# Expert gate and up weights in 4 KB rows, half the contraction of both in one slab, and 512-column projections

## The chip, the core and the metric

The kernel runs on one core of one Trainium2 chip. The metric is the device time of one execution in microseconds (us). The kernel before takes 1487.6 us (median of three runs, 1486.89 to 1495.12).

The engines: TensorE (PE, with its weight loads as PEld), VectorE (DVE), ScalarE (ACT), GpSimd (POOL), and SyncE (SP), which issues nearly all transfers from HBM.

## What is computed

Two transformer blocks on 256 tokens of width 1024, in float32. The change lies in the last stage of the second block, a mixture of 32 experts in 4 groups of 8. Each token goes to one group, and there to two experts. Cut to this stage:

```python
def hier_moe(h, w_rg, b_rg, w_re, b_re, w_gate, w_up, w_down):
    ...
    combine = jax.nn.one_hot(g_idx, N_EXPERT_GROUPS, dtype=jnp.float32)[:, :, None] * (g_w * within)[:, None, :]
    out = jnp.zeros_like(hf)
    for g in range(N_EXPERT_GROUPS):
        a = jnp.einsum('nd,edf->nef', hf, w_gate[g])
        u = jnp.einsum('nd,edf->nef', hf, w_up[g])
        act = jax.nn.silu(a) * u * combine[:, g, :, None]
        out = out + jnp.einsum('nef,efd->nd', act, w_down[g])
```

Per expert the gate and the up weights are 1024 x 256 each and the down weights 256 x 1024: three times 1 MB in float32. `h` is the RMS-normed input; its gain is `ffn_norm_2`.

## The kernel before

**Precision by splitting.** Every float32 operand of a large product is split into a high part and a rest (both in the fp32r format), and a product is three matmuls: high x high, high x low, low x high (`mm3`, L456). Activations are kept split already (`Uh`/`Ul`, here `SUh`/`SUl`). Weights are split as they arrive.

**The slab pipeline.** All weights of the program go through one ring of three slots (`NSLOT`), each slab 128 partitions x 2048 words (1 MB), in two halves of 1024 words:
- SP loads a half into `raw` (L406) when DVE has finished the half that was there before (the `lo_done` wait, L404).
- ACT copies it to `whi` (L418) when it has landed and when PE has used up the slab that was in the slot (the `slab_used` wait, L413).
- DVE subtracts, `wlo = raw - whi` (L424).
- PE waits for both halves of `lo_done`, multiplies, and counts up `slab_used`.

Each engine runs its own program in the written order, so a wait holds back everything behind it on that engine.

**The expert stage.** The tokens of a group are first gathered into at most 128 columns per group: PE multiplies the normed input (`XNh`, `XNl`, L2232) by 0/1 selection matrices, ACT and DVE scale by the gain and split the result into `SUh`/`SUl` (L1364, L1822). Then 32 experts follow, with the slabs in the order gate 0, up 0, gate 1, up 1, down 0, gate 2, up 2, down 1, and so on. For each step `body(E)` of the three engines does this, in this order:
- PE (`pe_experts`, L689): transposes the hidden vectors of expert E-1 (`turn`), projects the gate slab of E into bank 4 and its up slab into bank 5 (`project`, 8 chunks of the contraction x 3 matmuls of 256 columns each), then runs the down product of E-1 (`down`, 12 matmuls of 512 columns).
- ACT (`act_experts`, L754): SiLU of the gate projection of E (L778), split of gate E+1 and up E+1 (4 halves, L418), a copy of the transposed hidden vectors (`hh`, L791), split of down E (2 halves).
- DVE (`dve_experts`, L801): the product with up and combine weight (L814), the rests of gate E+1 and up E+1 (4 halves, L424), `hl` (L825), the rests of down E.

The SiLU of E waits for the gate slab alone, which PE finishes one slab before the up slab:

```python
                    act.wait_ge(*reach("slab_used", b + 3 * E))
...
                act.activation(sgh[:, 0, 0:T], bank[4][:, 0:T], ACT.Silu).then_inc(S("moe_silu"), 1)
                more = kind != 3
                if more:
                    split_hi(b + 2, E)
                    split_hi(b + 3, E)
```

Of every group of 8 experts, the first two steps are written out and the other steps run in a hardware loop (`runs`, L676; for the last group its last step is written out too). At the start of groups 2, 3 and 4 the finished group's result is copied out, multiplied by the transposed selection matrices (`put_back`, L714) and added to `X` by POOL (L840); the last group's follows at the end.

## Time and profile before

| | before |
|---|---|
| median of 3 runs | 1487.6 us (1486.89 to 1495.12) |
| span of the profiled execution | 1485.9 us |
| PE busy | 1369.9 us (92%) |
| DVE busy | 934.3 us (63%) |
| ACT busy | 766.2 us (52%) |
| read from HBM | 261.17 MB |

The span runs from the first to the last instruction; the profiled execution's own device time is not listed beside it, and the span is 1.7 us below the median of the three runs. PE is busy throughout, but the program has many stages with other limits. The expert stage fills the last 314 us of the span.

### The profile page before, as it was taken

What the parts mean: (1) busy time and instruction counts of PE and PEld (TensorE: products, weight loads), DVE (VectorE), ACT (ScalarE), POOL (GpSimd) and SP (SyncE); (2) the same over time, 40 slices, a digit from 0 to 9 for tenths busy, and PEclk for the clock granted to TensorE, in tenths of its full rate; (3) what the DMA queues carried; (4) which work ended last, traced back from release to release, by engine and by line L of the source; (5) the groups of instructions that cost most, each with busy time, mean ns of one, the idle gap of its engine ahead of it and who ended that gap; (6) DMA issues with size and microseconds to landing.
All of it is one profiled execution on the core that took longest, in us unless ns stands there. A gap on an engine that the chain in (4) does not pass through costs nothing.

```text
span 1485.9 us, 25448 instructions
## 1 busy us (share of the span) xinstructions
PE 1369.9 (92%) x9776; PEld 1273.7 (86%) x9776; DVE 934.3 (63%) x1359; ACT 766.2 (52%) x1112; POOL 175.3 (12%) x135
## 2 busy tenths in 40 slices
PE   6999999979989999998898987989998899999997
PEld 6999989977789999998897777889998788888885
DVE  4555554564565555564497663674664688888885
ACT  4343345645544343455454555325643577777774
POOL 1211120101002111200200001420000000202021
PEclk9999999999999999999998999989997899999999
DMA  7656554542155555554433232315453299999995
GB/s 241 214 182 192 178 146 156 158 141 78 58 170 168 178 191 181 186 156 120 135 114 114 85 110 64 112 40 162 157 171 128 85 338 347 321 343 322 336 322 189
DMA packets 222158, 263.36 MB, mean 177 GB/s; under 512 B 14017, under 2 KB 204798, under 8 KB 221950
## 3 DMA queue, kind: packets, MB, share of 16 engines
q1 hardware_dynamic: 219520, 260.39, 54.4%
q10 hardware_dynamic: 2558, 1.86, 0.4%
q8 instruction: 55, 0.90, 0.2%
q14 instruction: 25, 0.20, 0.0%
HBM read 261.17 MB, written 1.05 MB: 176 GB/s over the span
## 4 chain that ended last, share of the span: by engine, by line
PE 55%; issue 24%; DVE 11%; ACT 6%; POOL 2%; DMA 1%; ACTq 0%; POOLq 0%; DVEq 0%
PE bank L458 17%; PE bank L459 16%; PE bank L460 16%; DVE sb_wlo L424 3%; POOL sb_X L840 1%; ACT sb_whi L418 1%; DVE sb_XC L1580 1%; PE bank L2180 1%; PE bank L553 1%; ACT sb_aw L1256 1%; DMA sb_pos<-in_positions 1%; DVE sb_aw L1612 1%; DVE sb_st L862 1%; ACT sb_XC L1227 0%; ACT sb_xn L513 0%
## 5 line engine op out<-in xcount | busy, mean ns | idle before, releaser
L424 DVE TENSOR_TENSOR sb_wlo<-sb_raw,sb_whi 128x1024 fp32r<-128x1024 f32 (+1 forms) x498 | 620.3, 1289 | 252.4 <-ACT sb_whi L418 251.8
L418 ACT ACTIVATE sb_whi<-sb_raw 128x1024 fp32r<-128x1024 f32 (+1 forms) x498 | 503.6, 1047 | 305.3 <-PE bank L460 243.9
L458 PE MATMUL bank<-sb_Uh,sb_whi 128*128 128x256 f32 x1216 | 350.7, 288 | 6.0 <-DVE sb_wlo L424 4.5
L459 PE MATMUL bank<-sb_Ul,sb_whi 128*128 128x256 f32 x1216 | 347.6, 286 | 0.0
L460 PE MATMUL bank<-sb_Uh,sb_wlo 128*128 128x256 f32 x1216 | 347.4, 286 | 0.0
L458 PEld LDWEIGHTS bank<-sb_Uh,sb_whi 128*128 128x128 f32 x1216 | 237.3, 195 | 11.4 <-issue 8.3
L459 PEld LDWEIGHTS bank<-sb_Ul,sb_whi 128*128 128x128 f32 x1216 | 237.5, 195 | 0.7
L460 PEld LDWEIGHTS bank<-sb_Uh,sb_wlo 128*128 128x128 f32 x1216 | 236.9, 195 | 0.0
L458 PE MATMUL bank<-sb_whi,sb_Uh 128*128 128x256 f32 (+3 forms) x560 | 162.0, 289 | 1.2 <-DVE sb_Ul L543 0.8
L459 PE MATMUL bank<-sb_wlo,sb_Uh 128*128 128x256 f32 (+3 forms) x560 | 161.4, 288 | 0.0
L460 PE MATMUL bank<-sb_whi,sb_Ul 128*128 128x256 f32 (+3 forms) x560 | 161.3, 288 | 0.0
L458 PE MATMUL bank<-sb_whi,sb_SUh 128*128 128x256 f32 x512 | 148.4, 290 | 6.0 <-DVE sb_wlo L424 4.0
L459 PE MATMUL bank<-sb_wlo,sb_SUh 128*128 128x256 f32 x512 | 144.5, 282 | 0.0
L460 PE MATMUL bank<-sb_whi,sb_SUl 128*128 128x256 f32 x512 | 144.4, 282 | 0.0
L458 PE MATMUL bank<-sb_whi,sb_hh 128*128 128x512 f32 x288 | 113.1, 393 | 1.2 <-DVE sb_hl L825 0.9
L458 PEld LDWEIGHTS bank<-sb_whi,sb_Uh 128*128 128x128 f32 x560 | 111.6, 199 | 2.5 <-issue 1.9
L459 PE MATMUL bank<-sb_wlo,sb_hh 128*128 128x512 f32 x288 | 112.7, 391 | 0.0
L460 PE MATMUL bank<-sb_whi,sb_hl 128*128 128x512 f32 x288 | 112.3, 390 | 0.0
L459 PEld LDWEIGHTS bank<-sb_wlo,sb_Uh 128*128 128x128 f32 x560 | 111.7, 199 | 0.0
L460 PEld LDWEIGHTS bank<-sb_whi,sb_Ul 128*128 128x128 f32 x560 | 111.5, 199 | 0.0
L458 PEld LDWEIGHTS bank<-sb_whi,sb_SUh 128*128 128x128 f32 x512 | 97.1, 190 | 13.3 <-DVE sb_wlo L424 12.2
L460 PEld LDWEIGHTS bank<-sb_whi,sb_SUl 128*128 128x128 f32 x512 | 97.2, 190 | 0.0
(392 smaller groups left out, 1928.6 us busy)
## 6 DMA issues: line engine op xcount, KB each, us to landing
sb_raw<-in_w_in SPq DMA_DIRECT2D x104, 512.0 KB, 4.4
sb_raw<-in_ffn_w_in SPq DMA_DIRECT2D x88, 512.0 KB, 4.6
sb_raw<-in_w_gate SPq DMA_DIRECT2D x64, 512.0 KB, 4.7
sb_raw<-in_w_up SPq DMA_DIRECT2D x64, 512.0 KB, 6.4
sb_raw<-in_w_down SPq DMA_DIRECT2D x64, 512.0 KB, 6.1
sb_raw<-in_ffn_w_out SPq DMA_DIRECT2D x44, 512.0 KB, 3.7
sb_raw<-in_w_out SPq DMA_DIRECT2D x16, 512.0 KB, 4.5
sb_raw<-in_w_ssd_branch SPq DMA_DIRECT2D x16, 512.0 KB, 4.7
```

The costliest lines, as they stand in the source:

```text
L418: nc.scalar.activation(whi[:, i % NSLOT, c], raw[:, i % NSLOT, c], ACT.Copy).then_inc(S("hi_done"), 1)
L424: nc.vector.tensor_tensor(wlo[:, i % NSLOT, c], raw[:, i % NSLOT, c], whi[:, i % NSLOT, c].bitcast(F32), ALU.subtract).then_inc(S("lo_done ...
L458: pe.matmul(o, lh, rh, start=start, stop=False, skip_group_check=True)
L459: pe.matmul(o, lh, rl, start=False, stop=False, skip_group_check=True)
L460: return pe.matmul(o, ll, rh, start=False, stop=stop, skip_group_check=True)
L553: last = pe.transpose(bank[4 + j][:, c * T + t * P:c * T + (t + 1) * P], xn[:, t, (2 * j + c) * P:(2 * j + c + 1) * P], ident)
L840: pool.tensor_tensor(xs_, xs_, PUT[:, part], ALU.add).then_inc(S("x_add"), 1)
L862: dve.tensor_reduce(stat(nm, 2 * H)[:, t * H:(t + 1) * H], scr[:, 0:H * d].rearrange("p (h d) -> p h d", d=d), AX, ALU.add).then_inc(S(nm ...
L1256: act.activation(aw[:, i % 3, lo:hi], aw[:, i % 3, lo:hi], ACT.Exp, bias=nmx[:, 2 * i + t:2 * i + t + 1], scale=HD ** -0.5, accum_out=sm[: ...
L1580: dve.scalar_tensor_tensor(XC[:, ch, s_:T], sgh[:, j % 2, c * T:(c + 1) * T - s_], gcol("conv_w_2", (TAPS - 1 - s_) * NX + ch), XC[:, ch, ...
L1612: dve.tensor_tensor_reduce(out=aw[:, i % 3, lo:hi], in0=bank[i % 3][:, lo:hi], in1=SELB[:, lo:hi], scale=1.0, scalar=-3e38, op0=ALU.add, o ...
L2180: last = pe.matmul(bank[4 + v % 2][:, h * SP:(h + 1) * SP], EM(2 * v + h // 4)[:, h % 4 * P:(h % 4 + 1) * P], Xd[:, v % 2, h * SP:(h + 1) ...
```

## The change

- **Which rows of a weight go to which partition.** Before, chunk k of the contraction holds rows 128k to 128k+127, one per partition, so that a partition gets a 1 KB piece of each chunk. Now partition p gets rows 8p to 8p+7 (`(p k) n`), which lie together in HBM: 8 KB, read as two runs of 4 KB.
- **What a slab holds.** Before, one slab is a gate and the next is an up. Now the first slab holds chunks 0 to 3 of gate (first half) and up (second half), and the next slab chunks 4 to 7 of both. Sizes, slots, halves and their number stay.
- **The projections.** A matmul now streams 256 gate columns and 256 up columns together, 512 in all, into bank 4: 12 matmuls per slab instead of 24. Bank 5 is not used. Both results are complete only at the end of the second slab, so the SiLU waits for it (`slab_used` one higher).
- **The gathered input.** Its chunk c must now hold features c, 8+c, 16+c, ...: the stationary operand of the gathering matmuls is read with a step of 8 words (`every`). The gain is needed in the same order, so ACT loads it once more, early in the program, as 8 words per partition (one more transfer on its queue), and waits for it before it scales `SUh`.

The down weights and everything ahead of this stage stay as they were.

```diff
+        at_rows = P + n_rows2
+        row_gain = lambda c: G[:, at_rows + c:at_rows + c + 1]
...
-        experts = lambda nm, k: a[nm].rearrange("o g e (k p) n -> (o g e) p k n", p=P)
-        wg, wu, wd = (experts(nm, 0) for nm in ("w_gate_2", "w_up_2", "w_down_2"))
-        slab_loop("moe", NE, lambda e: wg[e], lambda e: wu[e], lambda e: wd[e])
+        wg, wu = (a[nm].rearrange("o g e (p k) n -> (o g e) p (k n)", p=P) for nm in ("w_gate_2", "w_up_2"))
+        wd = a["w_down_2"].rearrange("o g e (k p) n -> (o g e) p k n", p=P)
+
+        def rows_of(e, j):
+            c = slice(j * SLAB // 2, (j + 1) * SLAB // 2)
+            return [wg[e][:, c], wu[e][:, c]]
+
+        slab_loop("moe", NE, lambda e: rows_of(e, 0), lambda e: rows_of(e, 1), lambda e: wd[e])
...
+            if isinstance(src, list):
+                for h, half in enumerate(src):
+                    if i >= NSLOT or q is not None:
+                        n = h + 1 if part_cols(i) == part_cols(i - NSLOT) else 2
+                        sp.wait_ge(*reach("lo_done", 2 * (i - NSLOT) + n + (0 if q is None else q * 6)))
+                    sp.dma_start(raw[:, i % NSLOT, h * SLAB // 2:(h + 1) * SLAB // 2], half).then_inc(S(f"raw_full{i % NSLOT}{h}"), 16)
+                return
...
+        every = lambda x, c: x.rearrange("p (q k) -> p k q", k=KD)[:, c]
...
             def project(j, i, E, u):
                 pe.wait_ge(*reach("lo_done", 2 * (i + 1) + 6 * E))
-                by_token(i, 4 + j, SUh[:, :, u], SUl[:, :, u], KD, 256, tiles=[0]).then_inc(S("slab_used"), 1)
+                wh, wl = (w[:, i % NSLOT, :].rearrange("p (m k n) -> p k m n", m=2, n=EH) for w in (whi, wlo))
+                for k in range(KD // 2):
+                    c = j * KD // 2 + k
+                    last = mm3(bank[4][:, :], SUh[:, c, u], SUl[:, c, u], wh[:, k], wl[:, k], c == 0, c == KD - 1)
+                last.then_inc(S("slab_used"), 1)
...
-                if first:
-                    act.wait_ge(*reach("slab_used", b + 1))
-                else:
-                    act.wait_ge(*reach("slab_used", b + 3 * E))
+                act.wait_ge(*reach("slab_used", (b + 2) if first else b + 1 + 3 * E))
...
-                dve.scalar_tensor_tensor(sgh[:, 1, 0:T], sgh[:, 0, 0:T], w, bank[5][:, 0:T], ALU.mult,
+                dve.scalar_tensor_tensor(sgh[:, 1, 0:T], sgh[:, 0, 0:T], w, bank[4][:, T:2 * T], ALU.mult,
                                          ALU.mult).then_inc(S("moe_mul"), 1)
...
+            act.dma_start(G[:, at_rows:at_rows + KD], a["ffn_norm_2"][0].rearrange("(p k) -> p k", k=KD)).then_inc(S("ld_pb"), 16)
...
+            act.wait_ge(*reach("ld_pb", 16 * (len(pb_list) + 1)))
             for c in range(KD):
                 act.wait_ge(*reach("su_mm", c + 1))
                 act.activation(SUh[:, c].rearrange("p g n -> p (g n)"), bank[4 + c % 4][:, :], ACT.Copy,
-                               scale=gcol("ffn_norm_2", c)).then_inc(S("su_hi"), 1)
+                               scale=row_gain(c)).then_inc(S("su_hi"), 1)
...
-                        last = pe.matmul(bank[4 + c % 4][:, :], x_[:, t, c * P:(c + 1) * P], PICK[:, t, 0:EG].rearrange("p g n -> p (g n)"),
+                        last = pe.matmul(bank[4 + c % 4][:, :], every(x_[:, t], c), PICK[:, t, 0:EG].rearrange("p g n -> p (g n)"),
```

No instruction of ACT changes its place. ACT at the start of the expert stage before, from the SiLU of expert 0 to that of expert 1 (rows of three columns: line, operation with its tiles, semaphores waited for; L418 is the split):

```order
L778 ACTIVATE sb_sgh<-bank 128x256 [waits slab_used]
L418 ACTIVATE sb_whi<-sb_raw 128x1024 [waits raw_full20,slab_used]
L418 ACTIVATE sb_whi<-sb_raw 128x1024 [waits raw_full21]
L418 ACTIVATE sb_whi<-sb_raw 128x1024 [waits raw_full00,slab_used]
L418 ACTIVATE sb_whi<-sb_raw 128x1024 [waits raw_full01]
L791 ACTIVATE sb_hh<-bank 128x256 [waits moe_t]
L418 ACTIVATE sb_whi<-sb_raw 128x1024 [waits raw_full10,slab_used]
L418 ACTIVATE sb_whi<-sb_raw 128x1024 [waits raw_full11]
L778 ACTIVATE sb_sgh<-bank 128x256 [waits ffn_mul,slab_used]
```

The same place in the changed kernel:

```order
L796 ACTIVATE sb_sgh<-bank 128x256 [waits slab_used]
L433 ACTIVATE sb_whi<-sb_raw 128x1024 [waits raw_full20,slab_used]
L433 ACTIVATE sb_whi<-sb_raw 128x1024 [waits raw_full21]
L433 ACTIVATE sb_whi<-sb_raw 128x1024 [waits raw_full00,slab_used]
L433 ACTIVATE sb_whi<-sb_raw 128x1024 [waits raw_full01]
L809 ACTIVATE sb_hh<-bank 128x256 [waits moe_t]
L433 ACTIVATE sb_whi<-sb_raw 128x1024 [waits raw_full10,slab_used]
L433 ACTIVATE sb_whi<-sb_raw 128x1024 [waits raw_full11]
L796 ACTIVATE sb_sgh<-bank 128x256 [waits ffn_mul,slab_used]
```

The order is the same; what moved is the count of `slab_used` that the SiLU (the first and the last row) waits for, which is one higher, and the four splits stand behind it.

## Rows read from the trace of the kernel before

**Rows 1.** Page, section 2: DMA share of each of 40 slices, in tenths
```profile
DMA  7656554542155555554433232315453299999995
```

**Rows 2.** Stretches: length, busy PE, PEld, DVE, ACT, POOL, then PEclk, DMA, GB/s
```profile
1178.60:1182.00 3.40, 3.40 (x19) 3.40 (x18) 3.40 (x5) 0.04 (x1) 0.00 (x0) 0.51 0.78 270
...
1200.00:1470.00 270.00, 263.17 (x1802) 237.77 (x1800) 230.33 (x235) 204.89 (x248) 23.07 (x12) 1.00 0.95 329
```

**Rows 3.** Waits, 1165 to 1480 us: total us, times, longest
```profile
ACT sb_whi L418 <- DMA sb_raw<-in_w_up: 37.6, 58, 2.1
...
PEld bank L458 <- DVE sb_wlo L424: 12.6, 30, 2.1
```

**Rows 4.** Timeline of PE: start us, us, engine, line, operation [idle before <-releaser]
```profile
1178.01 0.39 PE L458 MATMUL bank<-sb_whi,sb_SUh 128*128 128x256 f32 x1 [1.83 <-DVE sb_wlo L424]
...
1460.50 0.38 PE L694 MATMUL bank<-sb_C,sb_sgh 128*128 128x128 f32 x2
1460.92 0.39 PE L458 MATMUL bank<-sb_whi,sb_SUh 128*128 128x256 f32 x1
...
1466.60 0.27 PE L460 MATMUL bank<-sb_whi,sb_SUl 128*128 128x256 f32 x1
1466.71 0.40 PE L458 MATMUL bank<-sb_whi,sb_hh 128*128 128x512 f32 x1
...
1469.44 0.38 PE L694 MATMUL bank<-sb_C,sb_sgh 128*128 128x128 f32 x2
```

**Rows 5.** Timeline of ACT: written-out steps first, then steps of the loop
```profile
1172.31 0.39 ACT L778 ACTIVATE sb_sgh<-bank 128x256 f32<-128x256 f32 x1 [2.08 <-PE bank L460]
1172.59 3.89 ACT L418 ACTIVATE sb_whi<-sb_raw 128x1024 fp32r<-128x1024 f32 x4
...
1220.02 0.36 ACT L778 ACTIVATE sb_sgh<-bank 128x256 f32<-128x256 f32 x1
1220.52 1.06 ACT L418 ACTIVATE sb_whi<-sb_raw 128x1024 fp32r<-128x1024 f32 x1
...
1462.30 2.26 ACT L418 ACTIVATE sb_whi<-sb_raw 128x1024 fp32r<-128x1024 f32 x2
```

**Rows 6.** Timeline of all engines: two hand-overs, and the last down product
```profile
1216.39 1.06 ACT L418 ACTIVATE sb_whi<-sb_raw 128x1024 fp32r<-128x1024 f32 x1 [0.40 <-DMA sb_raw<-in_w_up]
...
1217.48 1.23 DVE L424 TENSOR_TENSOR sb_wlo<-sb_raw,sb_whi 128x1024 fp32r<-128x1024 f32 x1 [0.23 <-ACT sb_whi L418]
...
1218.77 0.39 PE L458 MATMUL bank<-sb_whi,sb_SUh 128*128 128x256 f32 x1 [0.41 <-DVE sb_wlo L424]
...
1466.91 0.48 DVE L814 SCALAR_TENSOR_TENSOR sb_sgh<-sb_sgh,sb_CW,bank 128x256 f32<-128x256 f32 x1 [1.09 <-PE bank L460]
...
1470.28 0.42 DVE L825 TENSOR_TENSOR sb_hl<-bank,sb_hh 128x256 fp32r<-128x256 f32 x1 [0.62 <-ACT sb_hh L791]
...
1470.76 0.50 PE L458 MATMUL bank<-sb_whi,sb_hh 128*128 128x512 f32 x1 [0.93 <-DVE sb_hl L825]
```

**Rows 7.** Line L778, the SiLU: count, duration, first and last start
```profile
L778 ACT ACTIVATE sb_sgh<-bank x32: 359/366/390, 1172.3 to 1464.5; 128x256 f32<-128x256 f32 x32
```

**Rows 8.** Timeline at the end of group 1: copying out and putting back
```profile
1262.65 2.04 ACT L768 ACTIVATE sb_PUT<-bank 128x512 f32<-128x512 f32 x4
...
1263.29 0.50 PE L727 MATMUL bank<-sb_Yh,sb_PICKT 128*128 128x512 f32 x1 [1.58 <-ACT sb_PUT L768]
```

**Rows 9.** DMA view, 1209 to 1246 us: packets, MB, share of 16 engines; landing
```profile
q1 hardware_dynamic: 9776, 12.75, 99.3%
...
sb_raw<-in_w_up SPq DMA_DIRECT2D x9, 512.0 KB, 6.2
```

**Rows 10.** Groups by shape, 1130 to 1175 us: busy us, mean ns, idle before
```profile
L459 PEld LDWEIGHTS bank<-sb_wlo,sb_Uh 128*128 128x128 f32 x16 | 5.3, 333 | 0.0
...
L2232 PEld LDWEIGHTS bank<-sb_PICK,sb_XNh 128*128 128x128 f32 x16 | 3.8, 238 | 5.0 <-DVE sb_SUl L1822 2.1 <-DVE sb_PICK L1780 2.0
```

**Rows 11.** Line L1062 on ACT's queue: duration ns, first and last start us
```profile
L1062 ACTq DMA_DIRECT2D sb_PB<-in_q_norm x1: 1279/1279/1279, 21.6 to 21.6; - x1
```

More of the change, by code:

```diff
@@ L1028, in _ @@
             with sp.If(flag != 0):
-                load_experts(sp, over, EPG, lambda e: wg[first + e], lambda e: wu[first + e], lambda e: wd[first + e])
+                load_experts(sp, over, EPG, lambda e: rows_of(first + e, 0), lambda e: rows_of(first + e, 1), lambda e: wd[first + e])
                 sp.wait_ge(*reach("x_add", 4 * EG + 4))
@@ L1381, in _ @@
                     act.activation(SUh[:, c, 0], bank[4 + c // 4][:, c % 4 * P:(c % 4 + 1) * P], ACT.Copy,
-                                   scale=gcol("ffn_norm_2", c)).then_inc(S("su_hi"), 1)
+                                   scale=row_gain(c)).then_inc(S("su_hi"), 1)
                 split_hi(over)
@@ L1446, in _ @@
             lo_upto("kvup")
-            dve.wait_ge(*reach("ld_pb", 16 * len(pb_list)))
+            dve.wait_ge(*reach("ld_pb", 16 * (len(pb_list) + 1)))
             dve_head_sums("hq", MH, QK)
@@ L1821, in _ @@
                 dve.wait_ge(*reach("su_hi", c + 1))
-                dve.scalar_tensor_tensor(SUl[:, c].rearrange("p g n -> p (g n)"), bank[4 + c % 4][:, :], gcol("ffn_norm_2", c),
+                dve.scalar_tensor_tensor(SUl[:, c].rearrange("p g n -> p (g n)"), bank[4 + c % 4][:, :], row_gain(c),
                                          SUh[:, c].rearrange("p g n -> p (g n)").bitcast(F32), ALU.mult,
@@ L1830, in _ @@
                     dve.wait_ge(*reach("su_hi", KD + c // 4 * 4 + 4))
-                    dve.scalar_tensor_tensor(SUl[:, c, 0], bank[4 + c // 4][:, c % 4 * P:(c % 4 + 1) * P], gcol("ffn_norm_2", c),
+                    dve.scalar_tensor_tensor(SUl[:, c, 0], bank[4 + c // 4][:, c % 4 * P:(c % 4 + 1) * P], row_gain(c),
                                              SUh[:, c, 0].bitcast(F32), ALU.mult, ALU.subtract).then_inc(S("su_lo"), 1)
@@ L2258, in _ @@
                         for k, x_ in enumerate((XNh, XNl)):
-                            last = pe.matmul(bank[4 + c // 4][:, c % 4 * P:(c % 4 + 1) * P], x_[:, t, c * P:(c + 1) * P], PICK[:, t, EG],
+                            last = pe.matmul(bank[4 + c // 4][:, c % 4 * P:(c % 4 + 1) * P], every(x_[:, t], c), PICK[:, t, EG],
                                              start=c % 4 + t + k == 0, stop=t + k == 2, skip_group_check=True)
```

## The prediction, made before the changed kernel was run

> **What bounds the kernel now.** I read the page first, for the stage in which the change works. The DMA share stands at nine tenths or more in the last slices [rows 1], and that is the expert stage. Its stretches come next: from 1200 to 1470 us PE is busy 263.17 of 270 us, and the transfers 95% of the time [rows 2]. So the stage has two limits that lie close together, and the waits tell which ends last. ACT waits 37.6 us for up slabs [rows 3], but ACT is not what others wait for most: PE's largest wait is 12.6 us for DVE's rests [rows 3]. PE sets the pace, and late transfers add a little.
>
> One step of PE, from one transposition to the next, is 1460.50 to 1469.44 = 8.94 us [rows 4]: 0.42 for the transposition, 5.79 for the 48 projection matmuls of 256 columns (0.12 each), 2.73 for the 12 down matmuls of 512 (0.2275 each). Over the stage the 32 SiLUs start from 1172.3 to 1464.5 us [rows 7], 292.2 us for 31 steps. Of these PE's own work is 31 x 8.94 = 277.1, and three times eight put-back matmuls of 0.2275 are 5.5. The remaining 9.6 us are waits.
>
> The transfers: 12.75 MB in 99.3% of 37 us [rows 9] is 347 GB/s, so that one expert's 3.146 MB take 9.06 us, against steps of 9.42 on average. That is the case for the change: 4 KB rows may take this pressure off.
>
> **The change, part by part.**
>
> *The projections.* 24 matmuls of 512 at 0.2275 are 5.46, and the first after a wait lasts 0.11 longer (0.39 against the 0.28 of the others; 1460.92 shows it [rows 4]): 5.57 instead of 5.79. PE's own step falls to 0.42 + 5.57 + 2.73 = 8.72 us. This gives 0.22 us per step, 7 us in all, if PE stays the limit.
>
> *The wait of the SiLU.* This is the part that decides. ACT does, in this order, the SiLU of E and then the four splits of the next expert's two projection slabs. Before, the SiLU is released when the gate slab is done, and while PE projects the up slab ACT already splits the next one. Now the SiLU is released one slab later, at the end of both projections, and the splits stand behind it. PE's next projection needs the first slab split and its rests made. From the start of the last projection matmul the chain in the hardware loop is:
> - 0.40 until a 512-column matmul ends (1466.71 [rows 4]), 0.04 to the next engine (1466.87 to 1466.91 [rows 4, 6]);
> - 0.50 from the SiLU to the first split (1220.02 to 1220.52), 2.26 for two splits [rows 5];
> - 0.03 to DVE (1217.45 to 1217.48), 1.23 for the rest of the second half, 0.06 to PE (1218.71 to 1218.77) [rows 6].
>
> The sum is 4.52 us. In that time PE has 0.23 + 2.73 + 0.42 = 3.38 us of its own to do, so it idles 1.14 us in each step. From first to last projection matmul are 23 x 0.2275 + 0.11 = 5.34 us. The new step is **5.34 + 4.52 = 9.86 us**. In the written-out steps ACT is quicker: 0.28 to the first split, and four splits in 3.89, 0.97 apart, so two in 2.03 [rows 5]. The chain is 4.07 and the step 9.41.
>
> *The steps with a put-back* (three). PE's fourth part waits for ACT's first copy, behind the SiLU and four splits: 4.1 us of ACT [rows 5], 0.64 from that copy to PE [rows 8], then 0.56 for two matmuls, 0.42 for the transposition, 5.34 for the projections, 0.44 to the next SiLU: 11.50 us.
>
> *The sum of the stage.* 23 loop steps of 9.86 are 226.8, five written-out steps of 9.41 are 47.1, three of 11.50 are 34.5: 308.3 us between the first SiLU and the last. At the first step the trace shows a granted clock of 0.51, the 1.2 GHz level, for 3.4 us [rows 2], after PE had idled 1.83 us and gone on [rows 4]. The idle time there will be longer, so I take the same stretch again: half of 3.4 us is lost, 1.7. That is 310.0.
>
> *Its ends.* The first SiLU starts one half of the projections later, 1172.3 + 12 x 0.2275 = 1175.0, and the last at 1485.0. Today the last projections end at 1466.9 and the span at 1485.9, 19.0 later. The last down slab is now split after the SiLU: 0.50 + 2.26 + 0.03 + 1.23 = 4.0, then `hl` with 0.42 and the hand-over, 4.5 us where 3.85 stood (1466.91 to 1470.76 [rows 6]). So the span ends at 1485.0 + 19.0 + 0.6 = 1504.6, **18.7 us later** than 1485.9.
>
> *The transfers.* The larger rows should speed them up, but I cost that at nothing: even at today's 9.06 us per expert they are below 9.86. A half of a slot is free for its next load one step less one split and one rest, 9.86 - 1.06 - 1.23 = 7.6 us, and landing takes 6.2 under today's load [rows 9]. What hides them is the chain above. If that chain were gone, PE's 8.72 would be next and slower rows would cost 0.34 us a step. The ends for the unknown rate of the 4 KB rows are 347 GB/s and anything higher, and neither changes the sum.
>
> *The gathering matmuls* read their stationary operand with a step of 8 words. No row shows a load with a step. The nearest rows are the same loads without it, 238 ns in the mean with some at the slow clock, and a load at the slow clock, 333 ns [rows 10]. 32 loads of 333 ns, with a matmul that cannot run beside its own load, would space the pairs about 0.38 us apart instead of 0.2275: at most 32 x 0.15 = 4.8 us. A gain has no reason, since the same words are read. I take 0, because loads are hidden under 512-column matmuls today, and keep 4.8 for the range. The Trainium skill speaks against this part: its page "SBUF — State Buffer" (section "Door 1: The DMA port swizzle") says that SBUF has 16-byte lines and that an access which goes to a new line each time pays a penalty, which for float32 begins beyond 4 words; 8 words are beyond it. By that rule the sum would take up the 4.8 us instead of 0.
>
> *Small parts.* One more issue on ACT's queue, 1.3 us at the most of its ten neighbours [rows 11], stands before a wait of ACT for the angles and beside PE's long first product: 0. If that cover were gone, 1.3. The wait for that transfer before `SUh` comes 1,100 us later: 0. Reading 512 columns from two places of a slab, and one bank instead of two for SiLU and product: 0; bank 4 is read only after both slabs, and PE comes back to it after the transposition that needs the product anyway.
>
> The sum goes against the profiled execution, whose span is 1.7 us below the median of the runs. 18.7 us on the median give **1506.3 us**.
>
> **The rivals.**
> 1. *Faster: the chain does not bind.* The point is where the chain is below 3.38 us. Then PE's 8.72 rules and the late transfers vanish: 31 x 8.72 + 5.5 = 275.8 instead of 292.2, 1471 us. For it: ACT has room (205 of 270 us [rows 2]) and waits much for transfers. Against it: the chain is a sequence of single durations, and two splits, one rest and the SiLU alone are 0.50 + 2.26 + 1.23 = 3.99.
> 2. *No change within 0.5%.* That needs a chain of about 3.8 to 4.0, between this and the forecast: 1480 to 1495. Against it stands that hand-overs only add.
> 3. *Slower still by the step in the gathering loads.* The rule named above; 1506.3 + 4.8 = 1511.
> 4. *Slower still by the clock.* If PE's 1.14 us of idle time brought the lower level in each step as at 1178.6, 1.7 us a step would bring 50 us. Against it: the level is 1.00 from 1200 to 1470 with over 6 us of idle time spread there, single waits above 1 us among them [rows 2, 8].
> 5. *The change does not do what it says*, the transfers being no faster. It gives the forecast's time, since they are covered.
>
> A measurement of this kernel tells some 0.5% from no change, 7.4 us here.
>
> **How the numbers follow.** Forecast with the chain as priced: 0.68. Rival 3: 0.13. Rival 4, whole or in part: 0.04. Rival 1: 0.06. Rival 2: 0.09. If ACT ran the loop as fast as the written-out steps, 23 x 0.45 = 10.4 us would go, 1496; this is the low end of the forecast's own range. The high end is rival 3 and some more waiting for single late transfers: 1514. The range 1496 to 1514 leaves out rivals 1, 4 and most of 2. Faster by over 0.5%: 0.06. Within: 0.09. Slower, from the forecast and rivals 3 and 4: 0.85.
>
> **What would show it.** In the profile after: SiLUs about 9.9 us apart inside the loop; ACT's idle time before L418 no longer for transfers, its idle time before the SiLU for PE instead; PE waiting about 1.1 us in each step for DVE's rests, over 30 us in all; DMA share below nine tenths and fewer packets; the 512-column projections 0.23 us apart. I am wrong if PE waits little for the rests, if the DMA share stays at its top, or if a stage ahead of 1140 us changes.

## The result, and the profile after

| | before | after |
|---|---|---|
| median of 4 runs each | 1488.34 us (1486.89 to 1495.12) | 1509.76 us (1506.6 to 1513.29) |
| ratio of after to before | | 1.0145, 95% interval 1.0121 to 1.0169 |
| profiled execution: own time, span | span 1485.9 us | 1512.37 us, span 1510.6 us |

The change makes the kernel 1.4% slower. 1506.3 us was forecast, with a range of 1496 to 1514.

The rows of after stand in the order in which the prediction asked for them. Line numbers moved: the SiLU is now L796, the split L433, the rest L439, the project matmuls L473 to L475, the product L832, the transposition L711. The line of the SiLU first (duration, first and last start), which answers to [rows 7]:

```profile
L796 ACT ACTIVATE sb_sgh<-bank x32: 383/384/386, 1178.9 to 1490.5; 128x256 f32<-128x256 f32 x32
```

The 31 steps between take 311.6 us, where they took 292.2; 310.0 was forecast. The waits from 1165 to 1505 us (total us, times, longest), which answer to [rows 3]:

```profile
ACT sb_sgh L796 <- PE bank L475: 93.5, 32, 4.8
...
PEld bank L473 <- DVE sb_wlo L439: 36.2, 33, 2.5
PE bank L473 <- DVE sb_wlo L439: 27.5, 29, 2.3
...
ACT sb_whi L433 <- DMA sb_raw<-in_w_up: 5.0, 14, 0.9
```

ACT hardly waits for transfers any more (its waits for up slabs fell from 37.6 to 5.0 us). It waits for PE instead, 93.5 us before the 32 SiLUs, and PE waits for the rests once in each step. One step of the loop, in the timelines of ACT, DVE and PE (start us, us, operation, idle time before and what ended it):

```profile
1291.85 0.39 ACT L796 ACTIVATE sb_sgh<-bank 128x256 f32<-128x256 f32 x1 [3.42 <-PE bank L475]
1292.13 3.89 ACT L433 ACTIVATE sb_whi<-sb_raw 128x1024 fp32r<-128x1024 f32 x4
...
1293.21 4.63 DVE L439 TENSOR_TENSOR sb_wlo<-sb_raw,sb_whi 128x1024 fp32r<-128x1024 f32 x4 [0.36 <-ACT sb_whi L433]
...
1294.36 3.49 DVE L439 TENSOR_TENSOR sb_wlo<-sb_raw,sb_whi 128x1024 fp32r<-128x1024 f32 x3
...
1295.63 0.50 PE L473 MATMUL bank<-sb_whi,sb_SUh 128*128 128x512 f32 x1 [0.95 <-DVE sb_wlo L439]
...
1301.09 0.40 PE L475 MATMUL bank<-sb_whi,sb_SUl 128*128 128x512 f32 x1
...
1301.60 0.38 ACT L796 ACTIVATE sb_sgh<-bank 128x256 f32<-128x256 f32 x1 [3.14 <-PE bank L475]
```

(The second DVE row belongs to the first: it shows the same four rests from the second on, which starts at 1294.36.)

Read it as a loop of two legs. From the SiLU through the splits and the two rests of the first slab to PE's first projection: 1291.85 to 1295.63, 3.78 us. From there through 24 projection matmuls back to the next SiLU: 5.97 us. Together 9.75 us. Nothing else has to be late for a step to last that long.

The stretches (length, busy PE, PEld, DVE, ACT, POOL, PEclk, DMA, GB/s), which answer to the second of [rows 2], and the DMA view of 1209 to 1246 us, which answers to [rows 9]:

```profile
1200.00:1470.00 270.00, 243.62 (x1046) 190.76 (x1045) 218.06 (x222) 187.09 (x234) 23.19 (x12) 1.00 0.93 313
```

```profile
q1 hardware_dynamic: 3294, 11.98, 93.9%
...
sb_raw<-in_w_gate SPq DMA_DIRECT2D x8, 512.0 KB, 6.3
sb_raw<-in_w_down SPq DMA_DIRECT2D x7, 512.0 KB, 7.6
sb_raw<-in_w_up SPq DMA_DIRECT2D x7, 512.0 KB, 6.9
```

PE is busy 19.6 us less in the same 270 us, and the granted clock stays at 1.00, the 2.4 GHz level. There are a third as many packets, but 11.98 MB in 93.9% of 37 us is 345 GB/s, against 347 before. In this kernel the 4 KB rows move nothing faster.

**Where the 24.7 us between the two profiled spans lie.** 19.4 are the stage's 31 steps. 2.75 are its first half step: from the first projection to the first SiLU it is 5.87 us, where it was 3.12. The end gives back 1.3 (20.1 us from the last SiLU, where it was 21.4). Some 3.5 lie ahead of the gathering matmuls, which start at 1157.4 us where they started at 1153.9; in the profiled executions of the other kernels they start anywhere from 1147.7 to 1157.5, so this is scatter. 0.35 lie in the gathering matmuls themselves. So about 21 us belong to the change, as the medians say (21.4).

### The profile page after: what moved, and what is told of

Read it like the earlier page. It is cut to its first block, busy times and chain, and to the rows that moved or that the text cites. A ratio compares the mean times of both kernels' runs of the same rounds, so it can differ in the third digit from the quotient of the medians.

```text
span 1510.6 us, 23914 instructions
## 1 busy us (share of the span) xinstructions
PE 1373.8 (91%) x9008; PEld 1242.2 (82%) x9008; DVE 935.3 (62%) x1359; ACT 758.8 (50%) x1112; POOL 175.4 (12%) x135
## 4 chain that ended last, share of the span: by engine, by line
PE 56%; issue 25%; DVE 10%; ACT 6%; POOL 2%; DMA 1%; ACTq 0%; POOLq 0%; DVEq 0%
PE bank L473 17%; PE bank L474 17%; PE bank L475 17%; DVE sb_wlo L439 3%; POOL sb_X L858 1%; ACT sb_whi L433 1%; PE bank L2200 1%; DVE sb_XC L1600 1%; ACT sb_aw L1275 1%; DMA sb_pos<-in_positions 1%; PE bank L570 1%; ACT sb_xn L530 1%; DVE sb_st L880 1%; DVE sb_aw L1632 0%; ACT sb_sgh L875 0%
## 5 line engine op out<-in xcount | busy, mean ns | idle before, releaser
L439 DVE TENSOR_TENSOR sb_wlo<-sb_raw,sb_whi 128x1024 fp32r<-128x1024 f32 (+1 forms) x498 | 618.5, 1289 | 258.3 <-ACT sb_whi L433 257.7
L433 ACT ACTIVATE sb_whi<-sb_raw 128x1024 fp32r<-128x1024 f32 (+1 forms) x498 | 496.3, 1044 | 253.7 <-PE bank L475 243.8
L473 PE MATMUL bank<-sb_Uh,sb_whi 128*128 128x256 f32 x1216 | 352.6, 290 | 6.0 <-DVE sb_wlo L439 4.5
L475 PE MATMUL bank<-sb_Uh,sb_wlo 128*128 128x256 f32 x1216 | 349.2, 287 | 0.0
L473 PEld LDWEIGHTS bank<-sb_Uh,sb_whi 128*128 128x128 f32 x1216 | 239.1, 197 | 11.3 <-issue 9.2
L475 PEld LDWEIGHTS bank<-sb_Uh,sb_wlo 128*128 128x128 f32 x1216 | 238.8, 196 | 0.0
L473 PE MATMUL bank<-sb_whi,sb_Uh 128*128 128x256 f32 (+3 forms) x560 | 161.9, 289 | 1.2 <-DVE sb_Ul L560 0.8
L475 PE MATMUL bank<-sb_whi,sb_Ul 128*128 128x256 f32 (+3 forms) x560 | 161.1, 288 | 0.0
L473 PE MATMUL bank<-sb_whi,sb_SUh 128*128 128x512 f32 x256 | 105.4, 412 | 27.7 <-DVE sb_wlo L439 27.1
L473 PE MATMUL bank<-sb_whi,sb_hh 128*128 128x512 f32 x288 | 112.9, 392 | 1.7 <-DVE sb_hl L843 1.2
L473 PEld LDWEIGHTS bank<-sb_whi,sb_Uh 128*128 128x128 f32 x560 | 111.3, 199 | 2.5 <-issue 1.9
L475 PE MATMUL bank<-sb_whi,sb_hl 128*128 128x512 f32 x288 | 112.5, 391 | 0.0
L475 PEld LDWEIGHTS bank<-sb_whi,sb_Ul 128*128 128x128 f32 x560 | 111.3, 199 | 0.0
L475 PE MATMUL bank<-sb_whi,sb_SUl 128*128 128x512 f32 x256 | 101.8, 398 | 0.0
L474 PE MATMUL bank<-sb_wlo,sb_SUh 128*128 128x512 f32 x256 | 101.8, 398 | 0.0
L473 PEld LDWEIGHTS bank<-sb_whi,sb_SUh 128*128 128x128 f32 x256 | 48.5, 189 | 45.2 <-DVE sb_wlo L439 34.5
L858 POOL TENSOR_TENSOR sb_X<-sb_X,sb_PUT 128x512 f32<-128x512 f32 x16 | 28.1, 1788 | 340.8 <-ACT sb_PUT L789 340.8
```

The source lines that it names most:

```text
L433: nc.scalar.activation(whi[:, i % NSLOT, c], raw[:, i % NSLOT, c], ACT.Copy).then_inc(S("hi_done"), 1)
L439: nc.vector.tensor_tensor(wlo[:, i % NSLOT, c], raw[:, i % NSLOT, c], whi[:, i % NSLOT, c].bitcast(F32), ALU.subtract).then_inc(S("lo_done ...
L473: pe.matmul(o, lh, rh, start=start, stop=False, skip_group_check=True)
L474: pe.matmul(o, lh, rl, start=False, stop=False, skip_group_check=True)
L475: return pe.matmul(o, ll, rh, start=False, stop=stop, skip_group_check=True)
L858: pool.tensor_tensor(xs_, xs_, PUT[:, part], ALU.add).then_inc(S("x_add"), 1)
```

## The experiments

The question is what in the change costs the time, and why nothing of the hoped-for gain is seen. Theory W is that of the prediction: the late SiLU makes a round trip that sets the step. Its rivals put the cost on the rows, on the projections or on the transfers. All kernels of one section ran beside the kernel before on one chip.

### One part of the change at a time (before: 1486.25 us)

**e1_wait_only**: the kernel before, with the SiLU's wait of the change and nothing else.

```diff
-                if first:
-                    act.wait_ge(*reach("slab_used", b + 1))
-                else:
-                    act.wait_ge(*reach("slab_used", b + 3 * E))
+                act.wait_ge(*reach("slab_used", (b + 2) if first else b + 1 + 3 * E))
```

> The kernel before, with one edit: the SiLU waits until both projection slabs are used up, as in the change; rows, slabs and 256-column matmuls stay. Theory W (the later SiLU holds back the four splits behind it on ACT): with 48 matmuls of 0.118 us the step is 5.66 + 4.40 = 10.1 us, less the 0.1 by which the changed kernel's steps (9.76) were below the sum: about 10.0, so 31 x (10.0 - 9.42) = 18 us and 3 at the ends, 1505 to 1512 us. Rival D (rows, stride or 512-column matmuls cost the time): within 3 us of before, 1485 to 1491.

Measured: 1506.78 us (1505.62 to 1509.35), ratio 1.015 (1.0112 to 1.0187). Its waits from 1165 to 1505 us are those of the changed kernel:

```profile
ACT sb_sgh L775 <- PE bank L460: 102.0, 32, 6.4
...
PEld bank L458 <- DVE sb_wlo L424: 33.9, 30, 2.5
PE bank L458 <- DVE sb_wlo L424: 26.7, 29, 2.3
```

One wait, one slab later, makes the whole loss as far as the intervals can tell, with 1 KB rows, 256-column matmuls and plain loads untouched.

**e1_rows_only**: the changed kernel's rows, stepped loads and gains, but a gate slab and an up slab as before, 256-column projections into two banks, and the early SiLU (the part that sets the rows is shown).

```diff
-            c = slice(j * SLAB // 2, (j + 1) * SLAB // 2)
-            return [wg[e][:, c], wu[e][:, c]]
+            return [(wg, wu)[j][e][:, h * SLAB // 2:(h + 1) * SLAB // 2] for h in range(2)]
```

> The kernel before with the rows part alone: gate and up weights partition-major in 4 KB runs, the gathering loads with a step of 8 words and the gain in that order, but a gate slab and an up slab, 256-column projections into two banks and the early SiLU. Theory W says nothing is lost here; if the longer rows are faster, the transfer waits of ACT (over 50 us) and the 9.6 us by which the stage exceeds PE's own work shrink: 1478 to 1485. Rival D1 (rows of 4 KB at a distance of 8 KB are no faster, as the 345 GB/s at a share of 94% in the changed kernel hint): 1485 to 1491. Rival D2 (they are slower): above 1491.

Measured: 1487.12 us (1482.93 to 1490.88), ratio 1.0005 (0.9984 to 1.0025). The rows alone gain nothing and lose nothing, and the stepped loads cost nothing that shows.

**e1_proj_only**: the late SiLU, half-contraction slabs and 512-column projections, but 1 KB rows (`(k p) n`), plain loads and the old gains.

> The changed kernel with the rows as before: pieces of 1 KB, gathering loads without a step and the old gain columns; half the contraction of gate and up in a slab, 512-column projections and the late SiLU stay. Theory W: the rows are hidden, steps of 9.76 us as in the changed kernel, 1503 to 1511. Rival D (4 KB rows or the stepped loads cost the time): 1485 to 1495.

Measured: 1503.59 us (1502.66 to 1505.73), ratio 1.0127 (1.009 to 1.0164). That is 3 us below the wait alone, with intervals that overlap. The loop steps of the profiled executions are 9.76 us apart here and mostly 9.84 there, so the wider projections save under 0.1 us a step as long as the round trip sets it. (The one extra transfer of the gain is still issued in this kernel, and not used.)

### The splits ahead of the SiLU

If the round trip is the cause, the cure is to take the splits out of it. **e1_reorder** is the changed kernel with ACT's splits of the next first slab written ahead of the SiLU, and DVE's rests ahead of the product (ACT's part is shown):

```diff
                 first = isinstance(E, int) and E == 0
+                more = kind != 3
+                split_hi(*((b + 2, E) if more else (b + 3 * n - 1,)))
                 act.wait_ge(*reach("slab_used", (b + 2) if first else b + 1 + 3 * E))
...
-                more = kind != 3
                 if more:
-                    split_hi(b + 2, E)
                     split_hi(b + 3, E)
-                else:
-                    split_hi(b + 3 * n - 1)
```

> The changed kernel with one edit on ACT and one on DVE: the splits and the rests of the next expert's first slab stand ahead of the SiLU and of the product with up, instead of behind them. Theory W: PE's wait for the rests (about 1.1 us a step) goes, and the step is PE's 8.72 us or the transfers' 9.06, whichever is longer: 1472 to 1486, below before. Rival D (transfers are what slows it): the step stays near 9.7, 1500 to 1510.

Measured: 1500.01 us (1495.01 to 1502.87), ratio 1.0108 (1.0069 to 1.0148). Theory W's expectation failed: the time is the one that rival D named. The round trip is gone all the same (ACT's wait for PE before the SiLU fell from 93.5 to 5.9 us, PE's wait for the rests from 27.5 to 0.4), but something else took its place. Its waits from 1165 to 1505 us:

```profile
ACT sb_whi L433 <- DMA sb_raw<-in_w_gate: 42.9, 27, 2.7
PEld bank L711 <- DVE sb_sgh L832: 31.9, 24, 2.0
ACT sb_whi L433 <- DMA sb_raw<-in_w_up: 28.4, 56, 1.6
```

ACT now waits 71 us for transfers. The SiLU stands behind splits whose data are late, and PE's transposition waits for the product behind that SiLU. Two questions follow: are the 4 KB rows slow, and are they issued too late?

### The rows and the time of issue, with the splits first (before: 1486.35 us)

**e2_reorder_1k** is e1_reorder with 1 KB rows.

> Splits ahead of the SiLU (as in the run before, 1500.0 us), but with the old 1 KB rows. There the first half of a step's first slab landed 3.1 us after the half before it, the others 1.25 to 1.5. Theory T (what limits that kernel is the round trip of a slot: rest done, issue, landing, split; the rows matter little): 1 KB halves take 1.45 to 1.5 us instead of 1.27, at most 4 x 0.2 us a step, 1500 to 1525. Rival R (4 KB rows at a distance of 8 KB start slowly, and are themselves the 3.1 us): below 1495.

Measured: 1478.68 us (1475.4 to 1480.28), ratio 0.9932 (0.9906 to 0.9958). This is rival R's outcome, and theory T failed. The 4 KB rows cost 21 us in this order, although they cost nothing in e1_rows_only.

The time of issue: in the loop SP issues both halves of a step's first slab close together, since the first half too waits for both rests (`n = 2`, because `part_cols` compares this slab with the one ahead of the loop, which has another shape). SP's timeline of the changed kernel shows one slab's halves 0.42 us apart and the next slab's 1.00 us apart, about the time of one rest:

```profile
1295.77 0.33 SPq L412 DMA_DIRECT2D sb_raw<-in_w_gate  x1
1296.19 0.38 SPq L412 DMA_DIRECT2D sb_raw<-in_w_up  x1
1296.87 0.33 SPq L412 DMA_DIRECT2D sb_raw<-in_w_gate  x1
1297.87 0.33 SPq L412 DMA_DIRECT2D sb_raw<-in_w_up  x1
```

The edit lets the first half wait for its own rest alone:

```diff
-                        n = h + 1 if part_cols(i) == part_cols(i - NSLOT) else 2
+                        n = h + 1 if q is not None or part_cols(i) == part_cols(i - NSLOT) else 2
```

**e2_reorder_early** is e1_reorder with this edit.

> Splits ahead of the SiLU, 4 KB rows, and one edit on SP: inside the loops the first half of the first slab is loaded when the rest of its own half is done, not that of both halves (the condition compares with the router's slab, which is cut otherwise, so that today each loop step issues it 1.2 us late). Theory T (the round trip of the slots limits it): the step falls from 9.77 by 0.6 to 1.0 us towards PE's 8.72: 1470 to 1485. Rival R (the rate of the transfers limits it): 1495 to 1502, unchanged.

Measured: 1465.96 us (1462.86 to 1468.6), ratio 0.9862 (0.9833 to 0.9891). It beats both kernels and lies below theory T's range; rival R, which the run before had borne out, failed here. Its stretch, and its SiLUs:

```profile
1200.00:1450.00 250.00, 246.24 (x1088) 197.92 (x1086) 224.91 (x229) 194.11 (x240) 22.96 (x12) 1.00 0.93 340
```

```profile
L798 ACT ACTIVATE sb_sgh<-bank x32: 362/385/388, 1170.0 to 1442.4; 128x256 f32<-128x256 f32 x32
```

PE is busy 246 of 250 us. The 31 steps take 272.4 us. Why they are so short shows in the first load after the transposition, in the kernel before and here (start us, us):

```profile
1460.92 0.19 PEld L458 LDWEIGHTS bank<-sb_whi,sb_SUh 128*128 128x128 f32 x1 [0.28 <-DVE sb_wlo L424]
```

```profile
1302.21 0.38 PE L711 MATMUL bank<-sb_C,sb_sgh 128*128 128x128 f32 x2
...
1302.35 0.48 PE L473 MATMUL bank<-sb_whi,sb_SUh 128*128 128x512 f32 x1
```

Before, the projections follow 0.42 us behind the transposition, and 0.28 of that is a wait for DVE's rests; here they follow after 0.14. The loop steps are 8.54 us apart for the most part. In e2_before_early below they are mostly 8.97 or 8.98, and there too that wait stands in most steps. By these rows the splits' new place gives 0.28 of some 0.43 us a step, and the 512-column projections about 0.12 (5.67 us for 24 matmuls against 5.79 for 48). A kernel with the splits first and 256 columns was not run.

**e2_before_early** and **e2_rows_early** carry the same SP edit, on the kernel before and on e1_rows_only.

> The kernel before with the same edit on SP alone. Theory T: part of the 9.6 us by which the stage exceeds PE's own work goes: 3 to 8 us faster, 1479 to 1484 against 1487. Rival R (the rate of 1 KB rows is what makes transfers late): unchanged within 2 us.

Measured: 1478.32 us (1475.49 to 1486.48), ratio 0.9948 (0.9931 to 0.9966).

> The rows part alone (equal to before so far) with the same edit on SP. Theory T: with the round trip shortened the 4 KB rows can show their 1.27 us a half against 1.47: 4 to 9 us faster than before, at least as fast as the edit without them. Rival R (the rows are worth nothing in any case): the same as the edit without them, within 2 us.

Measured: 1483.38 us (1479.29 to 1489.25), ratio 0.9969 (0.9952 to 0.9987). A late issue of one half slab per step costs the kernel before some 8 us, as theory T said. Its second half failed: even with that late issue gone the 4 KB rows are no gain. 1483.4 against 1478.3 is probably a small loss: over ten runs each the means differ by 4.6 us, with a standard error of 1.4.

### Is it the late SiLU still, and is it the distance (before: 1486.81 us)

**e3_after_early** is the changed kernel with the SP edit alone.

> The changed kernel with one edit of SP's waits alone: the first half of a step's first slab is issued after one rest of its predecessor, not after both. The SiLU still waits for both slabs and the splits stand behind it. Theory W (the time of the changed kernel is set by the round trip of SiLU, splits and rest, and transfers are covered): 1505 to 1511 us, no change from 1509.8, loop steps still 9.76 us, although half slabs are issued earlier. Rival T (late transfers are a part of the changed kernel's loss): the edit gave 8 us in the kernel before and 34 us with the splits ahead of the SiLU, so at least 8 us should show here too: 1502 or less. Chances 0.85 and 0.15.

Measured: 1506.25 us (1502.9 to 1509.12), ratio 1.0134 (1.0102 to 1.0165), where the changed kernel has 1.0145. The same edit is worth 34 us with the splits first (e1_reorder against e2_reorder_early) and nothing that the medians can show with the SiLU first. Theory W stands: the loop steps are still 9.76 us, so the transfers are covered there. They are not quite covered in the steps with a put-back: the profiled executions have 12.69, 11.92 and 11.41 us for these in the changed kernel and 11.56, 11.49 and 11.37 here, and the 31 steps take 309.1 us instead of 311.6. In the loop the landing times fell and nobody gained by it (issues, KB, median us to landing, 1200 to 1450 us; first the changed kernel, then this one):

```profile
sb_raw<-in_w_gate SPq DMA_DIRECT2D x50, 512.0 KB, 6.2
sb_raw<-in_w_up SPq DMA_DIRECT2D x50, 512.0 KB, 6.8
```

```profile
sb_raw<-in_w_gate SPq DMA_DIRECT2D x50, 512.0 KB, 5.5
sb_raw<-in_w_up SPq DMA_DIRECT2D x50, 512.0 KB, 6.1
```

**e3_reorder_near** is e1_reorder with the contraction dealt out by halves, so that a half slab is one contiguous piece of HBM. The rows stay 4 KB long, but lie 4 KB apart instead of 8:

```diff
-        wg, wu = (a[nm].rearrange("o g e (p k) n -> (o g e) p (k n)", p=P) for nm in ("w_gate_2", "w_up_2"))
+        wg, wu = (a[nm].rearrange("o g e (j p k) n -> (o g e) j p (k n)", j=2, p=P) for nm in ("w_gate_2", "w_up_2"))
...
-            c = slice(j * SLAB // 2, (j + 1) * SLAB // 2)
-            return [wg[e][:, c], wu[e][:, c]]
+            return [wg[e][j], wu[e][j]]
...
-        every = lambda x, c: x.rearrange("p (q k) -> p k q", k=KD)[:, c]
+        every = lambda x, c: x.rearrange("p (j q k) -> p j k q", j=2, k=KD // 2)[:, c // 4, c % 4]
```

> As e1_reorder (splits and rests of the next first slab ahead of the SiLU and the product, 1500.0 us), but the contraction is dealt out otherwise: a half slab is one contiguous piece of 512 KB, in which partition p reads 4 KB at 4 KB distance, where it was 4 KB at 8 KB distance. The stationary operand of the gathering matmuls has a step of 4 words instead of 8. With 1 KB rows the same order took 1478.7 us. Theory D (the distance of 8 KB makes these transfers slow): 1480 us or less, waits of ACT for gate and up transfers below 40 us together. Theory K (4 KB rows as such land later in this order, whatever their distance): 1496 to 1504, waits as in e1_reorder (71 us together). Chances 0.4 and 0.5, 0.1 for something between.

Measured: 1476.44 us (1473.29 to 1481.64), ratio 0.993 (0.9906 to 0.9954). Theory D is right on the time, the less likely of the two by my chances: e1_reorder's 1500.0 is a matter of the 8 KB distance, not of 4 KB rows. The two kinds of waits that D put below 40 us together are 37.5 and 10.0, 47.5, so not all of it went. The stretch 1200 to 1450 us of e1_reorder, and of this kernel:

```profile
1200.00:1450.00 250.00, 227.79 (x979) 177.64 (x980) 207.01 (x209) 179.16 (x220) 23.26 (x12) 0.99 0.93 317
```

```profile
1200.00:1450.00 250.00, 242.08 (x1054) 190.56 (x1053) 220.42 (x222) 192.69 (x234) 22.81 (x12) 1.00 0.95 341
```

The transfers are busy 93% of the time in the one and move 317 GB/s, 95% in the other and 341: that is 341 against 359 GB/s of busy time. But the larger distance does not always mean this: e2_reorder_early has it too and moves 340 GB/s in 93%, 366 of busy time. One thing was edited beside the distance: the gathering loads have a step of 4 words instead of 8. They run ahead of the expert steps, and their own cost is small: 32 of them with a step of 8 took 0.35 us longer than without.

**e3_reorder_early_near** and **e3_reorder_early_1k** are e2_reorder_early with the other two kinds of rows.

> e2_reorder_early (splits first, 4 KB rows, early issue of the first half, 1466.0 us) with the contiguous half slabs of e3_reorder_near. Theory D (the distance of 8 KB costs something): 1455 to 1463 us. Theory K (the distance does not matter): 1463 to 1469. Chances 0.35 and 0.65.

Measured: 1466.39 us (1462.03 to 1470.09), ratio 0.9875 (0.984 to 0.9911).

> e2_reorder_early (1466.0 us) with the 1 KB rows of the kernel before, everything else the same: splits first, late SiLU, 512-column projections, early issue. Theory S (once the first half is issued early, the 4 KB rows are the quicker ones, 1.27 against 1.45 us per half slab): slower than 1466.0, 1470 to 1480. Theory N (both kinds move 3.1 MB in about 9 us and the size of the rows makes no difference): 1462 to 1469. Theory Q (4 KB rows cost time here too, as they did without the early issue, 21 us): 1450 to 1461. Chances 0.45, 0.35 and 0.2.

Measured: 1465.63 us (1464.73 to 1466.23), ratio 0.9865 (0.9841 to 0.9889). With the early issue all three kinds of rows give the same time, 1466 us. Theories K and N are right; theory S, to which I had given most, fails. PE is close to its limit in all three, so they could not show what quicker half slabs are worth. The stretch of the last kernel shows how near to its limit it is:

```profile
1200.00:1450.00 250.00, 246.76 (x1087) 197.53 (x1086) 226.76 (x228) 197.57 (x239) 23.03 (x12) 1.00 1.01 342
```

The DMA engines' share is 1.01 with 1 KB rows and 0.93 with 4 KB rows (e2_reorder_early), at the same 340 GB/s. So in this order 4 KB rows do leave room on the DMA engines, 8 points of their time, but PE is the limit and has no use for it. The 1 KB kernel gives 1466 us without any change to the rows, the gains used or the gathering loads.

**What stays open.** Why the 8 KB distance costs 24 us with the splits first (e1_reorder) and nothing with the early issue (e2_reorder_early) or in e1_rows_only. The early issue changes two things at once: the first half is released earlier, and the halves are no longer issued together. The runs don't separate the two, and they don't show which resource it is. In e1_rows_only two halves issued together are the two 4 KB pieces of the same 8 KB of one matrix, in e1_reorder they are pieces of two matrices with 4 KB between them unread. Whether that makes the difference was not tried. What speaks against issuing together as the whole cause: e3_after_early has the early issue, and its transfers still move only 316 GB/s at a share of 0.94 from 1200 to 1450 us, 336 of busy time. All kernels with 1 KB rows lie at 339 to 345 by that measure, the other ones with 4 KB rows at 355 to 370, and only the changed kernel (335), e3_after_early and e1_reorder (341) are as low.

## Why the prediction was right, point by point

- **The size** came out 18.7 us against 21.4 between the medians. The parts: 17.8 forecast for the 31 steps, 19.4 measured; 0.9 forecast for the two ends, 1.45 measured (2.75 less 1.3); 0 against 0.35 for the gathering.
- **The round trip** was the right mechanism. e1_wait_only shows it alone (1.015), and e3_after_early shows that the transfers do not set the loop step. The loop step was priced at 9.86 us and is 9.75 in the rows above, 9.76 to 9.85 in most others. That it came so close is in part luck, since errors offset each other. From SiLU to PE I had 0.50 + 2.26 + 0.03 + 1.23 + 0.06 = 4.08, and it is 3.78. The first split follows the SiLU after 0.28 when its data have long landed, and four splits take 3.89; I had taken the 0.50 and the 2.26 of steps [rows 5] in which ACT went through late transfers. And the path is another than I wrote. The second rest starts at 1294.36, when the second split has been done for about 0.2 us (it starts at 1293.08 and takes 1.06): it waits for DVE's own first rest. So the leg is 0.28, one split, two rests. From PE to the SiLU I had 5.78, and it is 5.97: the projection matmuls are 0.233 apart, not the 0.2275 of the down matmuls (last section), and the hand-over takes 0.11 instead of 0.04.
- **PE's own work in a step** was put too high. Of the 0.42 for the transposition 0.28 are a wait for the rests, as shown with e2_reorder_early, so that the same chain already cost a little in the kernel before. Without waits a step of the changed projections is 8.54 us and not 8.72. The forecast of the loop step did not need this term, because the chain outlasts it either way; rival 1 did.
- **The written-out steps** were put at 9.41; they are 9.67 to 9.69, and one is 9.97. Both legs are longer than priced: 3.78 against 3.63, since DVE's two rests set that leg here too, and 5.90 against 5.78.
- **The steps with a put-back** were priced at 11.50; they are 12.69, 11.92 and 11.41. What was missing in the first two are late transfers behind "four splits in 3.89": in the first, ACT waits for two late halves, and the first copy starts 5.39 us after the SiLU, not 4.1. With the halves issued earlier (e3_after_early) all three are near the price: 11.56, 11.49 and 11.37. Timeline of ACT at the first of them:

```profile
1269.41 0.38 ACT L796 ACTIVATE sb_sgh<-bank 128x256 f32<-128x256 f32 x1 [1.54 <-PE bank L475]
1269.69 2.20 ACT L433 ACTIVATE sb_whi<-sb_raw 128x1024 fp32r<-128x1024 f32 x2
1272.21 1.06 ACT L433 ACTIVATE sb_whi<-sb_raw 128x1024 fp32r<-128x1024 f32 x1 [0.32 <-DMA sb_raw<-in_w_gate]
1273.84 1.06 ACT L433 ACTIVATE sb_whi<-sb_raw 128x1024 fp32r<-128x1024 f32 x1 [0.56 <-DMA sb_raw<-in_w_up]
1274.80 2.04 ACT L789 ACTIVATE sb_PUT<-bank 128x512 f32<-128x512 f32 x4
```

- **The transfers**, costed at nothing, were covered, but with less to spare than I wrote. Under their new load they take 6.3 to 7.6 us to land, where I had put 6.2 against a slack of 7.6. What I said of the case without the chain was wrong in size: "slower rows would cost 0.34 us a step" rests on the steady rate alone. With the chain gone a step of e1_reorder takes 302.7 / 31 = 9.76 us on the average of all steps, and with the halves issued earlier (e2_reorder_early) 8.79: the time of issue counts, whatever the rate. The SiLUs of e1_reorder:

```profile
L798 ACT ACTIVATE sb_sgh<-bank x32: 361/366/388, 1171.7 to 1474.4; 128x256 f32<-128x256 f32 x32
```

- **A sign that did not come**: the DMA share was to fall below nine tenths, and "at its top" was to mean that I am wrong. It went from 0.95 to 0.93. The steps are longer, so less is moved per us (313 GB/s against 329), but less is moved per busy time too (337 against 346 GB/s, from the same rows). The kernel with the same steps and 1 KB rows, e1_proj_only, has a share of 0.91 from 1200 to 1450 us at the same 313 GB/s. The other signs came, PE's wait at 0.95 us in each step and 27.5 in all instead of over 30.
- **Rival 1** (1471 us, no chain) failed for this change. Its sum came close, 275.8 us for the stage against 272.4 in e2_reorder_early, and would have been closer with 8.54 for a step. What it lacked was two edits, the splits ahead of the SiLU and the early issue.
- **Rival 3** had the duration right and the price wrong. The gathering loads of the changed kernel, by their line (min, median, max ns, first and last start):

```profile
L2252 PEld LDWEIGHTS bank<-sb_PICK,sb_XNh x16: 313/330/337, 1157.4 to 1168.4; 128*128 128x128 f32 x16
```

  The kernel before has a median of 188 ns for the same loads. So the step does cost, as the Trainium skill's page "SBUF — State Buffer" (section "Door 1: The DMA port swizzle") says of accesses that go to a new 16-byte line each time. That the penalty begins beyond 4 words is not borne out for these loads: in e3_reorder_near, with a step of 4 words, their median is 317 ns. But the gathering as a whole lost only about 0.35 us, not 4.8. The slower loads run beside the matmuls all the same, where I had assumed that they cannot: in the changed kernel the matmuls of one stretch start 0.245 us apart (1162.04 to 1163.02 us), not 0.38, and 0.232 apart in the kernel before. And e1_rows_only, which has these loads too, shows no loss in the total.
- **Rival 4** (the clock) did not come. PE idles about 1 us in each step and the granted clock stays 1.00 from 1200 to 1470 us. Only the first step has a stretch at about half, as before, after PE had waited 1.08 and 2.29 us; that step is 11.01 us, and 9.41 + 1.7 = 11.11 was forecast:

```profile
1182.00:1185.40 3.40, 2.71 (x6) 2.16 (x7) 3.40 (x5) 3.24 (x5) 0.00 (x0) 0.54 0.37 116
```

- **"The transfers being no faster"** (rival 5) is what the changed kernel shows: 345 against 347 GB/s. The Trainium skill has the rule that I should have weighed: its page "DMA: Bandwidth & Descriptors" (section "Specifications") puts the smallest transfer for line rate at 512 bytes, and the 1 KB rows were above it already. The runs agree as far as the time goes, 1466 us with either kind of row, but PE is the limit there, and the DMA share in those two (1.01 and 0.93) says that the larger rows can take less of the engines' time.

## What to carry to other kernels

Before moving a wait later, write down the round trip that it closes: everything that stands behind the waiting instruction on its own engine until the waited-for engine gets its next input, against the work that engine has in the meantime. If the trip is longer, the difference is paid in each step, and a faster PE stage or a quicker transfer gives nothing until independent work is written ahead of the wait. Once it is, look at the issue times next: a condition on SP that released one half slab a rest too late was worth 8 us in the kernel before and 34 us in the reordered one, though only 13 and 10 with 1 KB rows or with rows at 4 KB distance.

## What the runs showed of the hardware that I had not expected

- 4 KB rows at 8 KB distance against the same at 4 KB distance: 1500.0 against 1476.4 us in one order of work, 1466.0 against 1466.4 in another. The long distance costs 24 us where two halves are issued together behind a late release, and nothing that shows where the first is issued earlier. Which of the two matters is open.
- With PE as the limit, 1 KB and 4 KB rows move the same 340 GB/s, at a DMA share of 1.01 and 0.93.
- Weight loads of 128x128 that read every fourth or every eighth word take 317 and 330 ns in the median, against 188 ns for words in a row (e3_reorder_near, the changed kernel, the kernel before), and 32 of them under 512-column matmuls cost only some 0.35 us.
- Projection matmuls that stream 256 gate and 256 up columns from two places of a slab are 0.233 us apart (1296.43 to 1301.09 us, 20 spacings), while the down matmuls with 512 columns in one piece are 0.2275 apart [rows 4]. Over 24 matmuls it is 0.13 us a step. The two places are not shown to be the cause: the put-back matmuls of the changed kernel read their 512 columns in one piece and are 0.234 apart, and the gathering matmuls of the kernel before, one piece too, 0.232.

```profile
1269.21 0.39 PE L748 MATMUL bank<-sb_Yh,sb_PICKT 128*128 128x512 f32 x1
...
1270.38 0.39 PE L749 MATMUL bank<-sb_Yl,sb_PICKT 128*128 128x512 f32 x1
```
